# A depthwise convolution on TensorE by sets of four 32-row matmuls instead of 128-row ones

## The reference

```python
def causal_dwconv(x, w, b):
    """Causal depthwise conv over positions. x (B,S,C), w (K,C), b (C,)."""
    k, c = w.shape
    y = lax.conv_general_dilated(
        x, w[:, None, :].astype(x.dtype),
        window_strides=(1,), padding=((k - 1, 0),),
        dimension_numbers=("NWC", "WIO", "NWC"),
        feature_group_count=c)
    return y + b

def conformer_conv_module(h, w_pw1, b_pw1, w_dw, b_dw, ln_g, ln_b, w_pw2, b_pw2):
    d = h.shape[-1]
    a = jnp.einsum("bsd,de->bse", h, w_pw1) + b_pw1
    u = a[..., :d] * jax.nn.sigmoid(a[..., d:])
    u = causal_dwconv(u, w_dw, b_dw)          # width 31
    u = jax.nn.silu(layernorm(u, ln_g, ln_b))
    return jnp.einsum("bsd,de->bse", u, w_pw2) + b_pw2
```

## Time and profile before

| | us |
|---|---|
| median of 3 runs | 949.61 |
| lowest and highest of them | 949.39, 950.07 |
| the profiled execution's own time | 950.07 |
| its span, first to last instruction | 948.3 |
| busy in the span: PE | 938.4 (99%) |
| DVE | 552.4 (58%) |
| ACT | 393.4 (41%) |
| POOL | 112.2 (12%) |

### The profile page before, as it was taken

One profiled execution on the slowest core, in us unless ns is written; L12 is line 12 of the kernel. 1 busy time (PEld: TensorE's weight loads), 2 busy tenths in 40 slices (PEclk: granted clock), 3 DMA queues, 4 the chain that ended last, 5 costly groups with the idle time before them and its releaser, 6 DMA issues.

```text
span 948.3 us, 11921 instructions
## 1 busy us (share of the span) xinstructions
PE 938.4 (99%) x4512; PEld 791.2 (83%) x4512; DVE 552.4 (58%) x703; ACT 393.4 (41%) x606; POOL 112.2 (12%) x74
## 2 busy tenths in 40 slices
PE   8999999999999999999999999999999999999997
PEld 6889899888888888888888898888888888888887
DVE  6899995657555555555434359765555655532333
ACT  7785596434333333332222355433333333322231
POOL 0558896000000000000000020000000000000000
PEclk9999999999999999999999999999999999999999
DMA  7320022233222222312232341233222232223212
GB/s 254 116 89 1 1 90 89 90 99 110 102 88 88 88 88 97 123 63 91 76 107 91 117 147 55 89 108 113 88 88 88 88 94 100 64 90 122 91 62 90
DMA packets 17020, 88.56 MB, mean 93 GB/s; under 512 B 2016, under 2 KB 4320, under 8 KB 9952
## 3 DMA queue, kind: packets, MB, share of 16 engines
q1 hardware_dynamic: 16416, 87.67, 27.2%
q10 hardware_dynamic: 576, 0.52, 0.2%
HBM read 86.09 MB, written 2.10 MB: 93 GB/s over the span
## 4 chain that ended last, share of the span: by engine, by line
PE 97%; DMA 1%; SPq 1%; DVE 0%; ACT 0%; issue 0%; DVEq 0%
PE bank L1138 29%; PE bank L1139 29%; PE bank L1140 29%; PE bank L1190 2%; PE bank L1191 2%; PE bank L1189 2%; DMA w_raw<-w_pw 1%; PE bank L1480 1%; PE bank L1224 1%; PE bank L1207 0%; PE bank L1448 0%; PE bank L1453 0%; PE bank L1452 0%; PE bank L1213 0%; PE bank L1342 0%; SPq L302 0%
## 5 line engine op out<-in xcount | busy, mean ns | idle before, releaser
L1138 PE MATMUL bank<-h_hi,w_hi 128*128 128x512 f32 x800 | 312.4, 390 | 1.4 <-DVE w_lo L768 1.4
L1140 PE MATMUL bank<-h_hi,w_lo 128*128 128x512 f32 x800 | 311.3, 389 | 0.0
L1139 PE MATMUL bank<-h_lo,w_hi 128*128 128x512 f32 x800 | 311.2, 389 | 0.0
L455 ACT ACTIVATE w_hi<-w_raw 128x2048 fp32r<-128x2048 f32 (+2 forms) x87 | 147.3, 1693 | 214.3 <-PE bank L1140 214.3
L768 DVE TENSOR_TENSOR w_lo<-w_raw,w_hi 128x2048 fp32r<-128x2048 f32 (+2 forms) x81 | 162.2, 2002 | 100.7 <-ACT w_hi L455 100.0
L1138 PEld LDWEIGHTS bank<-h_hi,w_hi 128*128 128x128 f32 x800 | 150.2, 188 | 33.5 <-DVE w_lo L768 1.8
L1139 PEld LDWEIGHTS bank<-h_lo,w_hi 128*128 128x128 f32 x800 | 150.2, 188 | 31.7 <-issue 0.5
L1140 PEld LDWEIGHTS bank<-h_hi,w_lo 128*128 128x128 f32 x800 | 150.2, 188 | 30.8
L1139 PE MATMUL bank<-u_lo,w_hi 128*128 128x512 f32 (+1 forms) x406 | 153.3, 378 | 0.0
L1138 PE MATMUL bank<-u_hi,w_hi 128*128 128x512 f32 (+1 forms) x374 | 141.0, 377 | 0.0
L1140 PE MATMUL bank<-u_hi,w_lo 128*128 128x512 f32 (+1 forms) x374 | 140.8, 377 | 0.0
(11 more groups left out here) (212 smaller groups left out, 1001.3 us busy)
## 6 DMA issues: line engine op xcount, KB each, us to landing
w_raw<-w_up SPq DMA_DIRECT2D x44, 1024.0 KB, 4.8
w_raw<-w_down SPq DMA_DIRECT2D x32, 704.0 KB, 4.0
w_raw<-w_pw SPq DMA_DIRECT2D x11, 1024.0 KB, 4.9
x_res<-x SPq DMA_DIRECT2D x3, 512.0 KB, 7.7
out<-out_sb SPq DMA_DIRECT2D x12, 128.0 KB, 1.9
w_raw<-w_pw SPq DMA_DIRECT2D x4, 256.0 KB, 7.7
w_raw<-w_pool SPq DMA_DIRECT2D x2, 512.0 KB, 3.7
band_raw<-band SPq DMA_DIRECT2D x1, 800.0 KB, 5.4
```

Of the source, the lines that this page charges most:

```text
L455: nc.scalar.activation(w_hi[s][:, 0:columns], w_raw[s][:, 0:columns], ACT.Copy).then_inc(w_rounded[s], 1)
L1138: M.matmul(dst, a, hi, start=start, stop=False)
L1139: M.matmul(dst, a, lo, start=False, stop=False)
L1140: return M.matmul(dst, b, hi, start=False, stop=stop)
```

## The change

The convolution of tiles 2, 3, 6 and 7 is done in another way. A matmul now has 32 rows: a quarter of a tile's channels (`quad`). Its 128 outputs are those 32 channels for two phases (even and odd output tokens) times two shares of the filter (the first 16 taps and the last 15). Its 264 columns are 256 token pairs and a lag of 8 by which the two shares stand apart. A tile takes 17 offsets x 3 passes x 4 quarters; the four quarters of one offset and pass stand one after another in PE's list, use different rows and write to four banks.

The outputs then lie in the wrong partitions. ACT drains the four banks into `stage`, and 16 transfers within SBUF per tile, 32 partitions x 256 elements each (`gather`), put the pieces in their places in `gathered`, the second share shifted by the lag; POOL adds the two shares into `conv_out` (`add_parts`). SP issues all transfers of tiles 2 and 3 and half of those of tiles 6 and 7; ACT issues the other half, after its drains.

Besides, the gate half of pw1 now comes first (slot 0), the value half second; all weight blocks are built once, early; DVE's shared taps are gone, as are the sums of several tiles on DVE and ACT: PE sums each late tile by itself. DVE subtracts the near mean from its two accumulators after tap 20 (`centre_sums`), and handles tile 7 before its last tap. The first pw2 weights load early; the second follow the gathers in SP's list.

```diff
 CONV_TILES, SUM_PAIRS = (2, 3, 6, 7), (0, 2)
-CONV_UNITS = 2 * len(CONV_TILES)
-SHIFTS = (TAPS + 1) // 2
+QUADS = 4
+QUAD = P // QUADS
+PHASES, PARTS_OF_TAPS = 2, 2
+HALF_TAPS = (TAPS + 1) // 2
+OFFSETS = HALF_TAPS + PHASES - 1
+SPAN = (PAD + T + 2) // PHASES
+TP = T // PHASES
+LAG = HALF_TAPS // PHASES
...
-BANKS_PW1 = [(0, 2), (6, 0), (2, 6), (2, 6)]
+BANKS_PW1 = [(0, 2), (6, 0), (2, 6), (6, 0)]
-BANKS_CONV = (0, 0, 1, 1, 0, 0, 1, 0)
+BANKS_CONV = ((0, 1, 2, 3), (2, 3, 6, 7), (0, 1, 2, 3), (6, 7, 0, 1))
...
+        def gather(queue, n, q):
+            for p in range(PHASES):
+                for h in range(PARTS_OF_TAPS):
+                    queue.dma_start(gathered[n][quad(q), h, PHASES - 1 - p, :], stage[n][quad(PARTS_OF_TAPS * p + h), q, LAG * h:LAG * h + TP]).then_inc(part_gathered[n], 16)
...
-            sp.wait_ge(conv_done, 5)
-            with sp.Fori(0, PW2_STEPS) as i:
-                load_step(w_pw2, 2 * i, M_PW2 + i, UNIT)
+            load_step(w_pw2, 0, M_PW2, UNIT)
+            for n in range(len(CONV_TILES)):
+                for q in range(QUADS if n < 2 else QUADS // 2):
+                    sp.wait_ge(even_drained, QUADS * n + q + 1)
+                    gather(sp, n, q)
+            load_step(w_pw2, 2, M_PW2 + 1, UNIT)
...
+            def add_parts(n):
+                pool.wait_ge(part_gathered[n], 16 * QUADS * PHASES * PARTS_OF_TAPS)
+                nc.gpsimd.tensor_tensor(by_phase(conv_out[:, CONV_TILES[n], :]), gathered[n][:, 0, :, :], gathered[n][:, 1, :, :], ADD).then_inc(conv_added, 1)
...
+                act.wait_ge(conv_done, n + 1)
+                if n in (1, 3):
+                    act.wait_ge(part_gathered[n - 1 - n // 3], 16 * QUADS * PHASES * PARTS_OF_TAPS)
+                for q in range(QUADS):
+                    nc.scalar.activation(stage[n][:, q, :], bank[BANKS_CONV[n][q]][:, 0:TP + LAG], ACT.Identity, bias=bias_out[:, q, n:n + 1]).then_inc(even_drained, 1)
+                if n >= 2:
+                    for q in range(QUADS // 2, QUADS):
+                        act.wait_ge(even_drained, QUADS * n + q + 1)
+                        gather(act, n, q)
...
+            taps(1, 14, CENTRED_AT)
+            centre_sums()
+            taps(1, CENTRED_AT, TAPS - 1)
+            dve.wait_ge(conv_added, 4)
+            V.tensor_tensor(conv_out[:, 7, :], conv_out[:, 7, :], near_mean, SUB).then_inc(dev_last, 1)
+            taps(1, TAPS - 1)
...
+            def conv_tile(n):
+                pe.wait_ge(hi_built, 1)
+                pe.wait_ge(lo_built, n + 1)
+                pe.wait_ge(even_rounded, n + 1)
+                pe.wait_ge(even_split, n + 1)
+                for m in range(OFFSETS):
+                    at_block = slice(n * ENTRIES + m * PARTS_OF_TAPS, n * ENTRIES + (m + PHASES) * PARTS_OF_TAPS)
+                    for w, x, first, final in ((block_hi, even_hi, m == 0, False), (block_hi, even_lo, False, False), (block_lo, even_hi, False, m == OFFSETS - 1)):
+                        for q in range(QUADS):
+                            last = M.matmul(bank[BANKS_CONV[n][q]][:, 0:TP + LAG], flat(w[quad(q), at_block, :]), x[quad(q), n, m % PHASES, m // PHASES:m // PHASES + TP + LAG], start=first, stop=final, skip_group_check=True)
+                last.then_inc(conv_done, 1)
...
+            conv_tile(0)
+            pw1_unit(3, 0)
+            pw1_unit(3, 1)
+            wait_drained((2, 3), DRAINED_PW1 + PW1_STEPS)
+            pe.wait_ge(near_copied, 1)
+            conv_tile(1)
+            for t in range(2):
+                pe.wait_ge(glu_done[t], PW1_STEPS)
+            pe.wait_ge(even_drained, QUADS + 2)
+            conv_tile(2)
+            pe.wait_ge(even_drained, 2 * QUADS + 2)
+            conv_tile(3)
```

More of the change, by code:

```diff
@@ L182, in build @@
[L182 to L188, removed]
@@ L374, in build @@
[L374 to L377 removed]
+                pool.wait_ge(even_rounded, n + 1)
+                nc.gpsimd.tensor_tensor(even_lo[:, n, :, :], by_phase(glu_even[:, n % 2, :]), as_f32(even_hi[:, n, :, :]), SUB).then_inc(even_split, 1)
@@ L533, in build_hi @@
-            def build_hi(u, first=0, last=UNIT_TAPS):
-                for k in range(first, last):
-                    block = nc.scalar.activation(conv_hi[u][:, k * HALF_CH:(k + 1) * HALF_CH], pair_mask[:, :], ACT.Copy, scale=tap_col[:, u, k:k + 1])
-                if last == UNIT_TAPS:
-                    block.then_inc(hi_by_act, 1)
+                for q in range(QUADS):
+                    nc.scalar.activation(quad_mask[quad(q), :], ident[quad(q), quad(q)], ACT.Copy).then_inc(mask_set, 1)
@@ new lines, in tap_columns, with build_hi @@
+                act.wait_ge(taps_copied, PARTS_OF_TAPS * len(CONV_TILES))
+                act.wait_ge(mask_set, QUADS)
+                nc.scalar.activation(tap_hi[:, :, :], tap_pad[:, :, :, :].rearrange("p n i h -> p n (i h)"), ACT.Copy).then_inc(taps_rounded, 1)
+            def build_hi(first, last):
+                for c in range(first, last):
+                    block = nc.scalar.activation(block_hi[:, :, c], tap_pad[:, :, :, :].rearrange("p n i h -> p (n i h)"), ACT.Copy, scale=quad_mask[:, c:c + 1])
+                if last == QUAD:
+                    block.then_inc(hi_built, 1)
@@ L601, in _ @@
             act.wait_ge(unit_done[1], M_PW1 + PW1_STEPS)
-            build_hi(7, last=UNIT_TAPS // 2)
-            drain_conv(1)
-            cross_even(3)
-            build_hi(7, first=UNIT_TAPS // 2)
-            def square_dev(c, dst, rows=slice(0, P)):
-                nc.scalar.activation(dst[rows, :], conv_out[rows, c, :], ACT.Square).then_inc(dev_squared, 1)
-            for c in range(4):
-                act.wait_ge(dev_early, c + 1)
-                square_dev(c, dev_sq[:, c, :])
-            drain_conv(2)
@@ new lines, in _ @@
+            pe.wait_ge(tap_step[0], SUM_STEPS)
+            sum_wide(conv_out[:, 4, :], start=False, stop=False, at_bank=BANK_DEV)
+            pe.wait_ge(tap_step[1], SUM_STEPS)
+            sum_wide(conv_out[:, 5, :], start=False, stop=True, at_bank=BANK_DEV).then_inc(dev_summed, 1)
+            for n in range(3):
+                pe.wait_ge(dev_squared, 6 + n)
+                last = sum_wide(dev_sq[:, (7, 4, 5)[n], :], start=False, stop=n == 2, at_bank=BANK_DEV_SQ)
+            last.then_inc(squares_summed, 1)
```

443 lines of the change are left out of this document (179 added, 264 removed).

## The result

The changed kernel takes 952.54 us (median of 12 runs, 950.96 to 957.35), the kernel before 949.99 us beside it (949.39 to 951.88). The ratio is 1.0037, with a 95% interval of 1.0020 to 1.0054: slower by 0.37%, where 948.5 us and "faster" were forecast. On a second chip the pair stood at 952.34 and 949.94, ratio 1.0030 (1.0017 to 1.0043). The runs before lie within 2.5 us, those after within 6.4. Three executions further down (one of pairs at 1345 us, two of early_sums at 1170 and 5335) and one of the kernel before (2451) lie far outside all others and count in no ratio and no range.

What follows compares the result with a forecast made beforehand. PE was taken as the bound, busy 99% of the span, with DVE and POOL near full in the convolution. The walk's -2.1 us plus 1.0 for the clock gave -1.1: 948.5 us, faster, range 945.0 to 959.5.

Steps and rivals of the forecast that it cites:

- the set of four: Four 32-row convolution matmuls on PE: taken at 0.123 us a set, 25.1 us in all against 43.9.
- Rival A: Convolution on PE: the four matmuls run side by side, 0.123 us a set; chance 0.64.
- B: Convolution on PE: weight loads not hidden, 0.18 us a set, end +5.5 us, 955.1; chance 0.15.
- C: Convolution on PE: bound by instruction issue, 0.24 us a set, end +17.6 us, 967; chance 0.07.
- D: Convolution on PE: the four matmuls go in turn, 0.48 us a set, end +67 us, 1016; chance 0.06.
- Steps 1 to 4: Walk through PE, DVE, ACT and POOL: tile 3 ends 111.2, tile 6 starts 116.4, tile 7 ends 130.2 us.
- The clock: PE's granted clock may fall after 5.2 us idle before tile 6: 1.0 us lost, bounds nothing to 6.3.
- steps 5 and 6: Tail behind tile 7: drains, transfers, shares added by 139.3, then DVE and five more sums; end 145.4 us, -2.1.
- the second set of pw2 weights ... costs nothing: Load behind the gathers on SP, at about 140 us: needed only some 20 us later, so no cost.
- Rival E: Transfers within SBUF slow, landing after 2.9 us and 0.6 apart: +0.9 us, 950.5; chance 0.08.
- so the transfers are late by 2.4 us, not the taps: Before the final sums: DVE's taps done at 136.9, tile 7's shares added only at 139.3 us.

Runs made afterwards that it cites:

- pairs: Changed kernel, SP waiting for tile 7's transfers before the pw2 weight loads, each tile 7 transfer carrying both phases in eight issues instead of sixteen; 952.66 us, ratio 1.0030.
- early_sums: value_early with PE's list in the order of its inputs and 13, 5, 8 and 7 fillers where PE was idle; 947.21 us, ratio 0.9975.
- again: The changed kernel without an edit, one run for a second trace; 958.74 us.
- drain_first: Changed kernel, with ACT draining tile 3 before it rounds the two tiles for the next convolutions; 954.63 us, ratio 1.0046.
- taps_first: Changed kernel, DVE's last two taps before its wait for tile 7, PE summing tiles 4 and 5 before 7, ten fillers removed; 950.10 us, ratio 1.0006.
- value_early: tail_hold with DVE draining the value of step 3 four taps earlier; 948.74 us, ratio 0.9989.
- sums: tail_hold with PE's list in the order its inputs come and fillers only where PE was idle; 949.40 us, ratio 0.9999.
- early_narrow: early_sums with the last seven channel sums as matmuls of one column instead of 128; 951.32 us, ratio 1.0013.
- tail_hold: taps_first, with SP also waiting for tile 7's transfers before it issues the pw2 weight loads; 950.41 us, ratio 1.0006.
- same_chip: The changed kernel without an edit, as yardstick beside other runs on one chip; 952.34 us, ratio 1.0030.

## Why the prediction was wrong

**Right: the set of four.** Rival A was the likeliest and holds: 0.125 us against 0.123; B (0.18), C (0.24) and D (0.48) are refuted by every tile at full clock. The Trainium skill's figure for four row tiles ("TensorE: Matmul & The Clock Gate", Part 3), which led to 0.19, does not hold for this set: the trace has 0.125 with its four loads, so nearly four times over one after the other. Steps 1 to 4 came out within a microsecond, the clock apart: tile 3 from 105.26 to 111.5 (104.9 to 111.2 forecast), tile 6 from 115.7 (116.4), the two drains between tiles 1.2, DVE's taps done at 136.3 (136.9).

**The clock** was in the sum with 1.0 and cost 1.5 us of tile 6 in the shortest run, 2.4 in a median one: a term that was under-sized, within its bounds.

**Wrong: the tail, steps 5 and 6.** The forecast let the end follow from the arrival of tile 7, added by 139.3, and had 145.4 for the sums, or 146.4 with the clock's 1.0. The traced end is 148.03, 1.6 more. In the trace ACT starts to drain 0.8 us late, behind a square and its own eight issues for tile 6, which take 0.80 each and not 0.47; the first of ACT's issues stands 1.24 after the drain's start instead of 2.0 (-0.8), the eight take 5.0 instead of 3.8 (+1.2), and the last lands 1.6 instead of 1.9 behind them (-0.3): arrival 0.9 late. The remaining 0.7 us are the step that was missing altogether: **PE's list**. The prediction counted only the sums behind the arrival (tile 7's own and five more) and put the 24 fillers and four sums that stand in PE's order between ACT's drain and them at nothing: 5.4 and 3.6 us of work. Since that list starts only when ACT has drained tile 7, it became the path: 14.45 us in all five traces in which the load did not catch a transfer and the list was as in the changed kernel, although the transfers moved by 2.3 us. The sentence "so the transfers are late by 2.4 us, not the taps" was right on the taps, but the third candidate for the end, PE itself, was not asked.

**Wrong: "the second set of pw2 weights ... costs nothing".** It is true for its own user and false for the queue's other users: issued just behind the transfers, it catches the last one in some runs. In the two traces that show it, it cost 4.2 us (again) and 2.9 (drain_first); that it is what made the other five long runs, at 956.0 to 957.4, is likely and not shown. Rival E had transfers of 2.9 us and 0.6 apart; the spacing came true, and 5.2 us of landing in some runs were beyond it.

**The sum.** Forecast -1.1; in the shortest run +0.5 at the end of the stage (0.9 for the span); in a median run +1.9 at the end of the stage, from more lost clock and a later start; with the caught transfer +8.3 in one trace. The range of 945.0 to 959.5 held the time. The gain that the change makes in PE's work was spent in three places: 4.2 us of pause before tile 6, 1.5 to 2.4 us of clock behind it, and a list that begins late. taps_first, value_early and sums give parts of these back, and early_sums gives them together: 5.1 us less than the changed kernel beside it.

What stays open: why the start of the program (pause and clock at 20 us) varies by 2.1 us between two runs of the changed kernel, and again between early_sums and early_narrow, while the runs of before lie within 3.3 us on all chips together (948.58 to 951.88); and why POOL's addition of tile 3 begins at 128.1 us in the first trace and at 131.2 in tail_hold's, where tile 3 ended only 0.7 us later (112.18 against 111.49).

## What to carry to other kernels

Before you price what arrives last, add up what the waiting engine itself still has in its order, fillers included, from the last event that it waits for: here 14.45 us of sums and fillers hid the whole gain of transfers that came 2.3 us sooner. Fillers that fitted an old order are work in a new one, and where the new order makes the engine idle they are missing. A large load that is issued behind small transfers must wait for them to have landed, else a race of 0.3 us between two queues costs 3 to 4.

## What the runs showed of the hardware

A transfer of 32 rows of 1 KB within SBUF costs its queue 0.59 to 0.61 us, 0.63 to 0.65 from start to start and the same with twice the bytes; with SP and ACT both issuing it is 0.7 to 0.8, and now and then an issue takes 1.2 to 1.7 us. In the first trace the four long ones of SP and ACT (at 117.6, 122.7, 127.8 and 131.7 us) each stand within 0.4 us of a 16 KB packet of the instruction queue; that the one makes the other was not tried. Before tile 6, PE's idle times of about 4 us were followed by a mean granted clock of 0.50 to 0.75 from 116 to 120 us. Shorter ones had either outcome: 0.77 to 0.80 after 1.9 us (early_narrow) and 2.2 (again) near 21 us, 0.59 and 0.68 after 2.3 (again) and 2.7 (value_early), but 1.00 after 2.6 us in drain_first and after 1.8 in same_chip and early_sums. With the last seven sums in matmuls of one column the clock fell to half with PE busy throughout; with 128 columns in the same place it stayed at 1.00.
